# A two-layer decoder trunk on one core: S5 with four input-matrix buffers, VectorE's subtractions later, GpSimd's first splits held, gate rows moved behind the convolution

## What is computed

```python
proj = u @ w_in                                   # layer 0
qkv_a, z_a, b_a, a_a, qkv_b = jnp.split(proj, ...)
qkv_a = jax.nn.silu(causal_depthwise_conv(qkv_a, conv_w))
beta = jax.nn.sigmoid(b_a)
g = -jnp.exp(a_log) * jax.nn.softplus(a_a + dt_bias)
...
h = u @ w_in                                      # layer 1, S5
bu_re, bu_im = einsum(bb_re, h), einsum(bb_im, h) # 64 groups of 16 channels, 64 states
x = associative_scan(a, bu)
y = einsum(c_re, x_re) - einsum(c_im, x_im) + d_skip * h
val, gate = jnp.split(jax.nn.gelu(y) @ w_glu, 2, axis=-1)
return val * jax.nn.sigmoid(gate)
```

## Time and profile before

| | us |
|---|---|
| runs, device time | 2837.51, 2840.11, 2839.8 |
| median | 2839.8 |
| profiled execution | 2842.4 |
| its span, first to last instruction | 2840.7 |
| mean granted clock of TensorE | 0.982 |

### The profile page before, as it was taken

The page is one execution under the profiler, slowest core; times in us unless marked ns, Lnnn a source line. Parts: engine busy times, 40 slices in busy tenths (PEclk is TensorE's granted clock), DMA queues, the critical chain, the costliest instruction groups (busy, mean ns, idle before and its releaser), DMA issues.

```text
span 2840.7 us, 44899 instructions
## 1 busy us (share of the span) xinstructions
PE 2731.4 (96%) x18169; PEld 2597.4 (91%) x18169; DVE 1250.5 (44%) x2137; ACT 615.9 (22%) x1085; POOL 1011.9 (36%) x462
## 2 busy tenths in 40 slices
PE   7999999999999999999999888899999999999997
PEld 6999888877999999999999787799899999999996
DVE  6655466656144444444432546710442322222234
ACT  4222333365141000000000331320420000000002
POOL 4444201033444444444443404144434444444440
PEclk9999999999999999999999998899999999999999
DMA  4235412020231222222222249741321111111102
GB/s 150 85 106 128 110 46 76 32 76 24 85 125 49 77 83 83 83 83 83 83 84 78 71 112 224 249 122 51 104 89 49 48 52 44 44 44 44 45 30 79
DMA packets 158150, 236.51 MB, mean 83 GB/s; under 512 B 57808, under 2 KB 120528, under 8 KB 155856
## 3 DMA queue, kind: packets, MB, share of 16 engines
q1 hardware_dynamic: 53552, 137.11, 15.6%
q10 hardware_dynamic: 104480, 97.71, 11.5%
HBM read 174.89 MB, written 64.09 MB: 84 GB/s over the span
## 4 chain that ended last, share of the span: by engine, by line
issue 36%; PE 32%; POOL 14%; DVE 7%; DMA 6%; ACT 3%; ACTq 1%; POOLq 0%; DVEq 0%; SPq 0%
POOL w_hi L727 9%; PE psum L769 6%; PE psum L770 6%; PE psum L771 6%; POOL w_lo L730 5%; DMA stage<-wstream 4%; PE psum L851 2%; DVE area L2271 2%; PE psum L1251 2%; PE psum L1225 1%; PE psum L1073 1%; DVE x_lo L2212 1%; PE psum L1094 1%; PE psum L1238 1%; DVE area L2268 1%
## 5 line engine op out<-in xcount | busy, mean ns | idle before, releaser
L769 PE MATMUL psum<-x_hi,w_hi 128*128 128x344 f32 (+2 forms) x3456 | 1129.6, 327 | 13.7 <-ACT area L1560 4.6
L770 PE MATMUL psum<-x_lo,w_hi 128*128 128x344 f32 (+2 forms) x3456 | 1110.0, 321 | 0.0
L771 PE MATMUL psum<-x_hi,w_lo 128*128 128x344 f32 (+2 forms) x3456 | 1108.3, 321 | 0.0
L727 POOL TENSOR_TENSOR w_hi<-stage,const 128x1024 fp32r<-128x1024 f32 x193 | 482.7, 2501 | 1604.1 <-PE psum L771 1491.2
L769 PEld LDWEIGHTS psum<-x_hi,w_hi 128*128 128x128 f32 x3456 | 653.3, 189 | 26.1 <-issue 8.6
L770 PEld LDWEIGHTS psum<-x_lo,w_hi 128*128 128x128 f32 x3456 | 653.2, 189 | 3.5 <-issue 1.7
L771 PEld LDWEIGHTS psum<-x_hi,w_lo 128*128 128x128 f32 x3456 | 652.6, 189 | 0.0
L730 POOL TENSOR_TENSOR w_lo<-stage,w_hi 128x1024 fp32r<-128x1024 f32 x193 | 484.9, 2512 | 15.1
L769 PE MATMUL psum<-act_hi,w_hi 128*128 128x344 f32 (+2 forms) x1056 | 344.0, 326 | 16.6 <-DVE area L2681 12.1
L2668 DVE TENSOR_TENSOR area<-area,psum 128x344 f32<-128x344 f32 (+2 forms) x132 | 67.7, 513 | 648.4 <-ACT area L1927 648.4
L771 PE MATMUL psum<-act_hi,w_lo 128*128 128x344 f32 (+2 forms) x1056 | 338.8, 321 | 0.0
(11 more groups left out here) (235 smaller groups left out, 2246.1 us busy)
## 6 DMA issues: line engine op xcount, KB each, us to landing
stage<-wstream SPq DMA_DIRECT2D x193, 512.0 KB, 3.5
s_set<-area ACTq DMA_DIRECT2D x8, 1860.0 KB, 7.8
proj<-area ACTq DMA_DIRECT2D x20, 520.0 KB, 2.7
area<-proj ACTq DMA_DIRECT2D x36, 256.0 KB, 3.9
resid<-area ACTq DMA_DIRECT2D x6, 1376.0 KB, 6.1
area<-resid ACTq DMA_DIRECT2D x6, 1376.0 KB, 9.1
area<-s SPq DMA_DIRECT2D x8, 1024.0 KB, 9.9
area<-s SPq DMA_DIRECT2D x8, 836.0 KB, 9.8
```

Source lines behind the costliest of these rows:

```text
L727: pool.tensor_tensor(per_block(w_hi[:, slot, :]), src, ones_block, ALU.mult).then_inc(high_split, 1)
L769: mm(out[:, 0:n], w_hi[:, slot, wk], hi[:, xk, a:a + n], start=first, stop=False)
L770: mm(out[:, 0:n], w_hi[:, slot, wk], lo[:, xk, a:a + n], start=False, stop=False)
L771: return mm(out[:, 0:n], w_lo[:, slot, wk], hi[:, xk, a:a + n], start=False, stop=last)
```

## The change

1. S5's input matrices get four buffers: the two old places and two new ones behind the state buffers. SyncE loads those of tiles 0 and 1 during the last norm of ffn0, ahead of the stage, those of 2 and 3 behind the set of tile 1, and those of tile m + 4 in `s5_tile(m)`. The loads of glu_a slabs 2 and 3 move behind `s5_tile(1)` and `s5_tile(3)`.
2. ScalarE copies outputs 3 before the first x_hi and the Gelu of tile 1, and does the Gelu and x_hi of tile 2 before it copies outputs 4. VectorE's x_lo of a tile come one or more scans later. TensorE does four instead of five glu steps before the outputs of tile 7.
3. GpSimd splits in_proj slabs 1 and 2 of the first round only when `x_ready` is at 4 and at 6.
4. The work on the gate rows moves behind the convolution loop, on ScalarE with an explicit load of its function table, and on VectorE.
5. In the tail `norm_root(4, 2, 0)` stands ahead of `norm_store(4, 1)`.

```diff
@@ -340,12 +340,14 @@
     z["x_pair"] = carve(at + 4 * QP * NJ, 2, QP, NJ + 1)
+    wins = [p.at, p.at + A_PH] + [4 * T + N_SET_A * s + A_WIN for s in range(2)]
+    z["win_all"] = [carve(w, A_PH - A_WIN) for w in wins]
+    z["win"] = [[carve(w + i * QP * P, QP, P) for i in range(2)] for w in wins]
     z["sets"] = []
...
         z["sets"].append({
-            "win": [carve(at + A_WIN + i * QP * P, QP, P) for i in range(2)],
             "ph": [carve(at + A_PH + i * QP * 144, QP, 144) for i in range(2)],
@@ -571,8 +573,8 @@
-                s = m % 2
-                sp.dma_start(z["a"][s][:, A_WIN:A_PH], s5_set[m][:, A_WIN:A_PH]).then_inc(s5[f"win_loaded{s}"], 16)
+                s = m % 4
+                sp.dma_start(z["win_all"][s], s5_set[m][:, A_WIN:A_PH]).then_inc(s5[f"win_loaded{s}"], 16)
@@ -612,7 +614,6 @@
-                load_win(m)
                 load_phases(m)
@@ -620,9 +621,10 @@
                 s = m % 2
+                if m + 4 < KT:
+                    sp.wait_ge(s5["v"], m + 1)
+                    load_win(m + 4)
                 if m + 2 < KT:
-                    sp.wait_ge(s5["v"], m + 1)
-                    load_win(m + 2)
                     sp.wait_ge(s5["x"], m + 1)
@@ -664,22 +666,27 @@
                     load(0)
+                    sp.wait_ge(s5["set_stored"], 16 * KT + 16)
+                    sp.wait_ge(x_ready, 14)
+                    load_win(0)
+                    load_win(1)
                     load(1, js=range(0, 2))
...
                     sp.wait_ge(x_ready, 18)
-                    sp.wait_ge(s5["set_stored"], 16 * KT + 16)
                     sp.wait_ge(s5["t_stored"], 16 * CH * KT)
...
                     s5_first_loads(1)
+                    load_win(2)
+                    load_win(3)
                     load_u(2)
...
                     load(0, js=range(0, 2))
-                    s5_tile(0)
-                    load(0, js=range(2, 4))
-                    for m in range(1, KT):
+                    for m in range(KT):
                         s5_tile(m)
+                        if m in (1, 3):
+                            load(0, js=range(2 + m // 2, 3 + m // 2))
                     load_y(KT - 1)
@@ -717,6 +724,8 @@
+                    if name == "in_proj" and before is None and j in (1, 2):
+                        pool.wait_ge(x_ready, 4 if j == 1 else 6)
                     per_block = lambda w: w.rearrange("p (k c) -> p k c", c=P)
@@ -1318,9 +1327,8 @@
-                s, turn = m % 2, m // 2
-                w = z["sets"][s]
-                pe.wait_ge(s5[f"win_loaded{s}"], 16 * (turn + 1))
+                win = z["win"][m % 4]
+                pe.wait_ge(s5[f"win_loaded{m % 4}"], 16 * (m // 4 + 1))
                 pe.wait_ge(s5[f"u_loaded{m % U_BUFS}"], (m // U_BUFS + 1) * 16)
@@ -1328,7 +1336,7 @@
                             o = bank[q][r, part * NJ:part * NJ + NJ]
-                            last = mm(o, w["win"][part][:, q, r], s5_u_in[m % U_BUFS][:, 2 * q + b, :], start=True, stop=True)
+                            last = mm(o, win[part][:, q, r], s5_u_in[m % U_BUFS][:, 2 * q + b, :], start=True, stop=True)
                 last.then_inc(s5["v"], 1)
@@ -1385,9 +1393,9 @@
             pe.wait_ge(s5["v_read"], KT + 1)
-            glu_steps((0, 1), range(0, 5))
+            glu_steps((0, 1), range(0, 4))
             s5_outputs(KT - 1)
-            glu_steps((0, 1), range(5, 6))
+            glu_steps((0, 1), range(4, 6))
             pe.wait_ge(group_free, 6 + GROUPS_BEFORE["glu_a"])
@@ -1521,15 +1529,6 @@
-            act.wait_ge(group_free, 6 + GATE_GROUPS)
-            tokens = slice(FRONT, T_ROWS)
-            ch(A(gb[0:4, tokens], ga[0:4, tokens], ACT.Abs))
-            ch.sync()
-            ch(A(gb[0:4, tokens], gb[0:4, tokens], ACT.Exp, scale=-1.0))
-            ch.sync()
-            A(gb[0:4, tokens], gb[0:4, tokens], ACT.Ln, bias=1.0).then_inc(gate_act, 1)
             cb, ct, po = conv_views(carve)
@@ -1564,6 +1563,14 @@
                 conv_tiles(i)
+            nc.scalar.preload_act_table_set("natural_log_exp_and_others")
+            act.wait_ge(group_free, 6 + GATE_GROUPS)
+            tokens = slice(FRONT, T_ROWS)
+            ch(A(gb[0:4, tokens], ga[0:4, tokens], ACT.Abs))
+            ch.sync()
+            ch(A(gb[0:4, tokens], gb[0:4, tokens], ACT.Exp, scale=-1.0))
+            ch.sync()
+            A(gb[0:4, tokens], gb[0:4, tokens], ACT.Ln, bias=1.0).then_inc(gate_act, 1)
             zeros = carve(18300, FRONT)
@@ -2006,8 +2013,8 @@
                     norm_square(4, 2, 0)
+                    norm_root(4, 2, 0)
                     norm_store(4, 1)
-                    norm_root(4, 2, 0)
                     norm_store(4, 2)
@@ -2111,10 +2118,13 @@
             ssm_late_evac(range(9, 12))
+            s5_out(3)
             s5_high(0)
...
             s5_high(1)
-            for m in range(3, KT):
+            s5_gelu(2)
+            s5_high(2)
+            for m in range(4, KT):
                 s5_out(m)
@@ -2242,21 +2252,6 @@
             ch.sync()
-            dve.wait_ge(gate_act, 1)
-            tokens = slice(FRONT, T_ROWS)
-            ch(V.tensor_scalar(rows[32:36, tokens], rows[32:36, tokens], 1.0, None, add))
-            ch.sync()
-            V.reciprocal(rows[32:36, tokens], rows[32:36, tokens]).then_inc(gate_dve, 1)
-            ch(V.scalar_tensor_tensor(out=ga[0:4, tokens], in0=ga[0:4, tokens], scalar=0.0, in1=gb[0:4, tokens],
-                                      op0=ALU.max, op1=add))
-            ch.sync()
-            ch(V.tensor_scalar(ga[0:4, tokens], ga[0:4, tokens], gate_col[0:4, :], -1.0, mul, mul))
-            ch.sync()
-            V.tensor_tensor_scan(rows[0:4, :], keep[0:4, :], ga[0:4, :], 0.0, mul, add).then_inc(gate_dve, 1)
             with dve.Fori(0, 3) as i:
@@ -2275,6 +2270,20 @@
             ch.leave(3)
+            dve.wait_ge(gate_act, 1)
+            tokens = slice(FRONT, T_ROWS)
+            ch(V.tensor_scalar(rows[32:36, tokens], rows[32:36, tokens], 1.0, None, add))
+            ch.sync()
+            V.reciprocal(rows[32:36, tokens], rows[32:36, tokens]).then_inc(gate_dve, 1)
+            ch(V.scalar_tensor_tensor(out=ga[0:4, tokens], in0=ga[0:4, tokens], scalar=0.0, in1=gb[0:4, tokens],
+                                      op0=ALU.max, op1=add))
+            ch.sync()
+            ch(V.tensor_scalar(ga[0:4, tokens], ga[0:4, tokens], gate_col[0:4, :], -1.0, mul, mul))
+            ch.sync()
+            V.tensor_tensor_scan(rows[0:4, :], keep[0:4, :], ga[0:4, :], 0.0, mul, add).then_inc(gate_dve, 1)
@@ -2846,7 +2855,7 @@
             gelu_out = [z["yg"], spare_slots[1][:, 0:SEQ]]
-            LOWS_BEHIND = {4: (0, 1), 5: (2, 3), 6: (4,), 7: (5, 6, 7)}
+            LOWS_BEHIND = {4: (0,), 5: (1,), 6: (2, 3), 7: (4, 5, 6, 7)}
```

2 lines of the change are left out of this document (1 added, 1 removed).

## The result

| | before | after |
|---|---|---|
| median of four runs, us | 2839.95 | 2809.5 (2808.1 to 2814.8) |
| profiled execution, us | 2842.4 | 2814.8 |
| its span, us | 2840.7 | 2813.0 |

The ratio is 0.9892 (95%: 0.9871 to 0.9914), some 30 us; 2811 had been forecast. The total is right; not all of its terms are. I go through the places in order of time.

A forecast was written before the change was run, and what follows sets the result against it. TensorE, busy 96% of the span, was taken as the bound, so only its waits count. Terms 7.5 + 6.1 - 3.3 + 15.9 + 2.9 = 29.1 us off 2839.8 gave 2811 us, own range 2803 to 2817, overall 2803 to 2825.

The forecast's parts named there:

- 1. The opening: Opening: with GpSimd's splits of slabs 1 and 2 held back, VectorE's first subtractions run free; gain 7.5 us.
- 2. The gate rows out of the opening: End of convolution: without VectorE's gate rows, TensorE's wait for tile 1's banks and its low clock go; gain 6.1 us.
- 3. Behind the convolution: Behind the convolution: three gate-row activations delay ScalarE's evacuation of the next tile, TensorE's wait grows; loss 3.3 us.
- The case with a load more: Behind the convolution: if the second table load stays, the loss is 4.6 us, or 6.0 by the skill page.
- 4a. u(0): S5, first half: less of set 0 ahead of the store shortens the first states' wait for u(0); gain 2.5 us.
- 4b. The matrices of tile 3: S5, first half: loads issued 50 us earlier remove TensorE's wait for tile 3's matrices and its low clock; gain 6.9 us.
- 5. The second half: S5 after outputs 3: VectorE is the longer chain, fewer subtractions stand ahead of scan 6; gain 6.5 us, between 1 and 10.
- rival B: S5's second half stays bound by loads y(2), u(6), y(3), u(7) behind a later Gelu: 2821 us, chance 0.23.
- Rival D: S5: ScalarE's small stores of u are starved, u(4) to u(7) each come 10 us late: 2851 us, chance 0.05.
- 6. The tail: Tail: with ScalarE's root for cut 2 ahead of the store, VectorE's idle time before the last scaling goes; gain 2.9 us.
- Rival C: S5: low clock hardly falls as waits get shorter than 2 us, 6 to 8 us more gain: 2804 us, chance 0.08.

The follow-up runs named there:

- E1: Kernel before with only the two holds on GpSimd's splits of in_proj slabs 1 and 2: 2821.8 us, ratio 0.9969.
- E2: Kernel before with only the gate rows moved behind the convolution, on ScalarE and VectorE: 2825.5 us, ratio 0.9983.
- E4: Kernel before with only the tail edit, the root for cut 2 ahead of the store of cut 1: 2828.3 us, ratio 0.9996.
- E12: Kernel before with only VectorE's changed order of subtractions and four glu steps instead of five ahead of outputs 7: 2822.0 us, ratio 0.9969.
- E5: The changed kernel unaltered, run once more on chip 11: 2811.6 us, ratio to the kernel before 0.9928.
- E3: Kernel before with all edits inside S5 and nothing else: 2818.8 us, ratio 0.9965.
- E10: Changed kernel with ScalarE's evacuation of tile 12 directly behind the convolution, ahead of the gate rows: 2796.9 us, ratio to the kernel before 0.9884.
- E9: Changed kernel with the input matrices of tiles 2 to 7 loaded late again, into the four buffers: 2806.1 us, ratio to the kernel before 0.9911.
- E8: Changed kernel with VectorE's subtractions in the order of before: 2812.5 us, ratio to the kernel before 0.9936.
- E11: E10 plus five buffers for ScalarE's late copies and ScalarE's old order in S5: 2798.3 us, ratio to the kernel before 0.9877.

## Why the forecast held, point by point

**1. The opening, 7.5:** 7.5 in the first pair of traces, 7.4 in E1. The row at the earlier trace rows gave 1.55 us for a subtraction with GpSimd idle, and the second and later ones ran at that. The page "SBUF — State Buffer" of the Trainium skill (section "SBUF: two separate sides") has VectorE, in an instruction with two inputs in SBUF, and GpSimd, in one that reads SBUF, hold a shared port pair as an exclusive lock for a whole instruction. The rows here agree, with 0.69 us growing to 2.88 beside a split.

**2. The gate rows out of the opening, 6.1:** 6.1 in the pair, 6.5 alone. That the holds alone would shorten the same wait (by 1.7, and half its low clock) wasn't in the sum; it makes the parts overlap by 2.6, but not the total wrong, as the sum was made for both.

**3. Behind the convolution, -3.3:** -2.4 in the pair, -2.2 in E2. From the last convolution Silu to the first evacuation of a z tile ScalarE takes 2.5 us more (187.51 to 207.60, 201.12 to 218.70 before), less than the three activations' 3.3, as the DMA issues begin while the third still runs. VectorE's gate rows delayed nothing, as forecast. The case with a load more didn't come; the load took 1.28 again.

**4a. u(0), 2.5:** 3.8 in the pair, but the wait of 5.4 us that it starts from was that of one execution: the other four traces with the old loads show 1.0 to 2.0 (E1, E2, E4, E12). With the early matrices it is 1.6 in the first trace and nothing in the eight others, and u(0) lands 4.0 to 5.0 us after its issue in these eight, where it took 5.6 to 6.7 in the four. So its reason holds, and it is worth 1 to 2 us.

**4b. The matrices of tile 3, 6.9:** 13.9 in the pair. Four traces of the old S5 have a first half of 86.2, 84.5, 80.9 and 80.6 us (before, E1, E2, E4; E12, with the same first half, 83.7), four of the new one 72.3, 79.9, 73.0 and 72.1 (the first, E5, E3, E10). The means, 83.0 and 74.3, differ by 8.7. The mechanism holds (E9 pays 4.2 when the loads are late again), but it is only half of the difference; which edit gives the rest wasn't tried.

**5. The second half, 6.5:** in the same traces the old S5 takes 72.9, 74.4, 74.1 and 74.8 (mean 74.1), the new one 75.7, 73.3, 69.8 and 68.1 (mean 71.7): 2.3, near the low end of 1 to 10, and -2.8 in the pair. VectorE's order is worth more than the step had for all: 9.4 where it is the only edit (E12, 64.7), and 8.0 where it alone is undone (E8, 79.7). By E12's one trace the other edits of S5 take back some 7. The chain that the step worked out is what E12 shows: scans 6 and 7 start at +16.5 and +28.9, and outputs 7, forecast to end at +44, are copied at +44.8. The step that failed is "SyncE's load of y(2) waits for it, u(6) behind that": u(6) was put at +10.9 and came at +16.0 in the first trace, +11.8 in E5, and the text stopped there. The phases of tile 6 stand in the same queue behind both and land at +20 to +24 instead of +14, and scan 6 begins with them. The second half goes with that landing: 64.7 us with +13.8 (E12), 66.1 with +15.9 (E11), 69.8 with +19.9 (E3), 68.1 with +20.3 (E10), 73.3 with +20.8 (E5), 75.7 with +23.9 (the first). That the phases alone make these lengths isn't shown: in no run do they go ahead of y(2) in the queue. It was rival B's mechanism, a load released late, at a load that neither B nor the forecast named.

**Rival D**, the starved stores, is real and doesn't decide. The store that took 4.3 us before (issued at 1782.2) takes 24.3 in the first trace after, and ScalarE stands for it. But these buffers have slack: the stand cost TensorE 3.7 us at outputs 4 and moved the Gelu of tile 1, and with it the phases of tile 6, some 4 us behind E5's, where outputs 4 waited 0.3; it is one of the reasons why this second half is the longest. The case needed 7 us lateness at each of four loads of u. The page "DMA: Bandwidth & Descriptors" (section "Queues, rings and completion order") has the engines take turns packet by packet; by that a small store should only be slowed while another queue is busy, and 24.3 us at a DMA share near 1.0 can still be that, as SyncE's queue was never empty. No run here tells turns from a queue that is shut out.

**6. The tail, 2.9:** 3.0.

**Rival C**, less low clock: in the pair it did vanish in S5's first half (0.90 to 1.00) and grew in the second (0.86 to 0.80); in E3, E5 and E10 the second half is at 0.88, 0.86 and 0.90, against 0.84 to 0.86 with the old S5.

Then the total, in which luck has a part. In the first pair S5's two halves missed by 7.0 one way and by 9.3 the other (13.9 for 6.9, -2.8 for 6.5), and the errors nearly cancel. Nor does the gain stay at 30 us: in E5 it is 20. Summed by their ratios on chip 0, the four parts give 8.8, 4.8, 9.9 and 1.1, 24.6 less the overlap of 2.6: 22. The kernel before is 6 to 10 us faster in the later comparisons and the changed one isn't. In the traces of E1, E2 and E4 the old S5 with its wait for u(0) takes 5 to 8 us less than in the trace of before. Another 3 to 4 lie in layer 0's mixer, which no edit touches: the trace of before has 13.65 us at 0.50 of the clock there (from 582.86), these three 3.4 to 6.8, but the first trace of the changed kernel has the 13.65 too. The forecast was made from an execution whose S5 had more low clock in its first half than any of the four later traces with the old loads, and its terms 4a and 4b took that as given. Against E5 its gain of 29 is 9 us too high. Why the old code meets more low clock in one comparison than in another, chip or occasion, these runs don't show.

## What to carry to other kernels

When an instruction is moved later, follow every load that its queue holds behind the one that waits for it, to the last: here two loads behind the Gelu, y(2) and u(6), were followed, and the fifth, the phases, is what the next scan waited for. A wait of a stage that lives at a DMA share of 0.9 to 1.0 is one draw: compare the stage's length in several traces before a wait of 5 us becomes a term of a sum. And look for work of the same table set that can go ahead of moved work: one moved line (E10) gave about as much as the holds or all of S5's edits.

## What the runs showed of the hardware that I hadn't expected

- The same program has its low-clock stretches in other places from one execution to the next: the first half of S5 ran at 0.90, 0.96, 0.98, 0.98 and 0.94 of the clock with the same old loads (before, E1, E2, E4, E12).
- Where GpSimd begins to split a slab 1.0 us ahead of VectorE's four instructions (E5) instead of 1.3 behind the first (E10), it turned into 3.4 us of wait and 10.24 us at half clock: 7 us of S5's first half in E5, and again in E11.
- The issue of one DMA held ScalarE's queue for long while the DMA engines were full (share 1.01 over the first half). The first store of y took 10.20 us to issue in the first trace after, 5.3 to 7.3 in the eight others with the new S5, 0.3 to 3.6 with the old, where the later stores of y mostly take 0.34:

```profile
1729.22 10.20 ACTq L2096 DMA_DIRECT2D s_y<-area  x1
1739.52 0.81 ACT L2062 ACTIVATE spare_slots<-psum 128x344 f32<-128x344 f32 x1 [10.33 <-issue]
```
- A wait of 9.5 us of the busiest engine cost next to nothing (E9): the load for which the next scan waited landed only 0.5 us before it ended.
